# A hybrid mixer layer on one core: the head regrouped into four pairs of channel blocks, with its loads, transposes and low parts reordered

## The reference, cut to what matters

```python
c_act = jax.nn.silu(c)
mod = (c_act @ w_mod + b_mod)[:, None, :]            # 1024 -> 6 x 1024
sh_m, sc_m, gt_m, sh_f, sc_f, gt_f = jnp.split(mod, 6, axis=-1)
h = rms_norm(x, g_pre_mix) * (1.0 + sc_m) + sh_m
y = hybrid_mixer(h, w_in, ...)                       # proj = h @ w_in, 1024 -> 7 x 1024, then conv, LRU, gates, w_o
x = x + gt_m * rms_norm(y, g_post_mix)
# then a squared-ReLU MLP of 4096 channels, treated in the same way
```

## Time and profile before

| what | value |
|---|---|
| runs | 834.62, 836.40, 836.66 us |
| profiled execution | 835.04 us, of which span 833.3 us |
| granted TensorE clock, mean | 0.992 |
| busy: TensorE, weight load, VectorE, ScalarE, GpSimd | 813.3, 701.9, 507.5, 440.0, 28.3 us |
| DMA | 109.52 MB, mean 131 GB/s |

### The profile page before, as it was taken

The page is one execution under the profiler, slowest core; times in us unless marked ns, Lnnn a source line. Parts: engine busy times, 40 slices in busy tenths (PEclk is TensorE's granted clock), DMA queues, the critical chain, the costliest instruction groups (busy, mean ns, idle before and its releaser), DMA issues.

```text
span 833.3 us, 12458 instructions
## 1 busy us (share of the span) xinstructions
PE 813.3 (98%) x4270; PEld 701.9 (84%) x4270; DVE 507.5 (61%) x682; ACT 440.0 (53%) x650; POOL 28.3 (3%) x24
## 2 busy tenths in 40 slices
PE   6799999999999999999999999999999999999997
PEld 6588888888888888888888899999999888888885
DVE  4746677656685565566675579777777533333335
ACT  6356777766674444444334566676767622333332
POOL 1542000000000000000000000000000000000000
PEclk9899999999999999999999999999999999999999
DMA  9942333326077666667337031333333532223302
GB/s 290 348 130 82 107 108 107 107 82 182 26 210 219 181 197 201 189 177 209 129 101 253 1 101 44 109 102 101 101 101 101 177 101 96 85 96 101 101 0 101
DMA packets 134943, 109.52 MB, mean 131 GB/s; under 512 B 4460, under 2 KB 119300, under 8 KB 134916
## 3 DMA queue, kind: packets, MB, share of 16 engines
q1 hardware_dynamic: 134740, 109.10, 43.8%
q10 hardware_dynamic: 144, 0.04, 0.0%
q0 software_dynamic: 32, 0.02, 0.0%
HBM read 107.04 MB, written 2.10 MB: 131 GB/s over the span
## 4 chain that ended last, share of the span: by engine, by line
PE 97%; DVE 1%; ACT 1%; POOL 0%; issue 0%; DMA 0%; DVEq 0%; ACTq 0%
PE ps L416 32%; PE ps L417 31%; PE ps L418 31%; PE ps L1460 1%; PE ps L1471 0%; PE ps L1607 0%; PE ps L1483 0%; POOL ht_lo L600 0%; ACT xnt L657 0%; ACT ht_hi L659 0%; PE ps L1579 0%; PE ps L1580 0%; PE ps L1491 0%; DMA crows<-in_c_dram 0%; DVE sums L1331 0%
## 5 line engine op out<-in xcount | busy, mean ns | idle before, releaser
L416 PE MATMUL ps<-ht_hi,w_hi 128*128 128x512 f32 x448 | 176.9, 395 | 8.0 <-POOL ht_lo L600 5.2
L417 PE MATMUL ps<-ht_lo,w_hi 128*128 128x512 f32 x448 | 175.8, 392 | 0.0
L418 PE MATMUL ps<-ht_hi,w_lo 128*128 128x512 f32 x448 | 175.6, 392 | 0.0
L1020 DVE TENSOR_TENSOR w_lo<-raw,w_hi 128x1024 fp32r<-128x1024 f32 x100 | 122.0, 1224 | 56.7 <-ACT w_hi L630 54.9
L630 ACT ACTIVATE w_hi<-raw 128x1024 fp32r<-128x1024 f32 x96 | 100.4, 1049 | 33.3 <-PE ps L418 28.7
L416 PEld LDWEIGHTS ps<-ht_hi,w_hi 128*128 128x128 f32 x448 | 84.9, 189 | 27.2 <-issue 9.5
L418 PEld LDWEIGHTS ps<-ht_hi,w_lo 128*128 128x128 f32 x448 | 84.9, 190 | 18.0
L417 PEld LDWEIGHTS ps<-ht_lo,w_hi 128*128 128x128 f32 x448 | 85.1, 190 | 17.5
L416 PE MATMUL ps<-w_hi,hd_hi 128*128 128x512 f32 x256 | 99.6, 389 | 0.0
L417 PE MATMUL ps<-w_lo,hd_hi 128*128 128x512 f32 x256 | 99.6, 389 | 0.0
L418 PE MATMUL ps<-w_hi,hd_lo 128*128 128x512 f32 x256 | 99.6, 389 | 0.0
(11 more groups left out here) (227 smaller groups left out, 1492.9 us busy)
## 6 DMA issues: line engine op xcount, KB each, us to landing
raw<-in_w_in_dram SPq DMA_DIRECT2D x48, 512.0 KB, 4.8
modraw<-in_w_mod_dram SPq DMA_DIRECT2D x32, 512.0 KB, 4.0
raw<-in_w_mlp_down_dram SPq DMA_DIRECT2D x32, 512.0 KB, 3.3
up_raw<-in_w_mlp_up_dram SPq DMA_DIRECT2D x56, 256.0 KB, 3.4
mod_raw<-in_w_mod_dram SPq DMA_DIRECT2D x32, 256.0 KB, 7.0
xs<-in_x_dram SPq DMA_DIRECT2D x8, 512.0 KB, 5.3
raw<-in_w_a_out_dram SPq DMA_DIRECT2D x8, 512.0 KB, 5.4
raw<-in_w_b_out_dram SPq DMA_DIRECT2D x8, 512.0 KB, 5.5
```

The source lines that it names most:

```text
L416: nc.tensor.matmul(dst, l_hi, r_hi, start=first, stop=False, skip_group_check=chained)
L417: nc.tensor.matmul(dst, l_hi, r_lo, start=False, stop=False, skip_group_check=chained)
L418: return nc.tensor.matmul(dst, l_lo, r_hi, start=False, stop=last, skip_group_check=chained)
L1020: V.tensor_tensor(w_lo[:, slot, :], raw[:, slot, :], f(w_hi[:, slot, :]), ALU.subtract).then_inc(w_lo_ready, 1)
```

## The change

The groups become four pairs. Every block's unit weights are loaded, rounded and split alone, and lie between the chunks of the modulation. TensorE takes row blocks 0 to 3 of group 0 straight from the chunks, in between the transposes of x, and VectorE 4 to 7. x is first transposed into six banks; blocks 6 and 7 follow in banks 4 and 5 when these have been copied out. Blocks 0 and 1 are modulated straight from PSUM. VectorE makes the low part of the first block of each group. It accumulates a group only when it has finished with the group before. The vectors are all loaded by SP behind x. ScalarE runs a sigmoid and a square root on one column ahead of the data. The unread transposes between tiles go, and 14 come ahead of the first product.

```diff
-    GROUPS = ((0,), (1,), (2, 3), (4, 5), (6, 7))
+    GROUPS = ((0, 1), (2, 3), (4, 5), (6, 7))
+    PE_ROWS = 4
...
+        X_BANKS = 6
+        X_LATE = {6: 4, 7: 5}
...
-                    if g0 == 0 and m0 > 0:
-                        sp_eng.wait_ge(mod0_sum, 1)
+                    if g0 == 0 and m0 < PE_ROWS:
+                        sp_eng.wait_ge(mod0_rows, m0 + num0)
...
             for t in range(TB):
                 sp_eng.dma_start(xs[:, t, :], x_v[:, t, :]).then_inc(xr_in[t], 16)
-                if t == 0:
-                    load_vectors(sp_eng, vectors[1::2], vec_in)
-            load_mod0_group(0)
+            load_vectors(sp_eng, vectors, vec_in)
+            per_group = len(CHUNKS) // len(GROUPS)
+            for c in range(per_group):
+                load_mod0(c)
             load_first_units(0)
-            load_first_units(1)
-            load_mod0_group(1)
-            for g in range(2, len(GROUPS)):
-                load_first_units(g)
-                load_mod0_group(g)
+            for g in range(1, len(GROUPS)):
+                for i in range(per_group):
+                    load_mod0(g * per_group + i)
+                    if i == 1:
+                        load_first_units(GROUPS[g - 1][1])
+                    if i == 2:
+                        load_first_units(GROUPS[g][0])
+            load_first_units(NB - 1)
...
(GpSimd)
             first_units_lo(0)
             pool.wait_ge(h_lo, 1)
+            input_lo(1)
+            first_units_lo(1)
             for g in range(1, len(GROUPS)):
-                first_units_lo(g)
-                for k in GROUPS[g]:
-                    input_lo(k)
+                k0, k1 = GROUPS[g]
+                first_units_lo(k0)
+                pool.wait_ge(h_lo, k0 + 1)
+                input_lo(k1)
+                first_units_lo(k1)
...
(ScalarE)
-            load_vectors(act, vectors[0::2], vec_in)
+            act.wait_ge(const_ready, 4)
+            A(ysum[:, 3 * TB - 1:3 * TB], eps_t[:, 0:1], ACT.Sigmoid)
             act.wait_ge(c_sum, 1)
             A(c_act[:, :], ps[:, B_T0, 0:NB], ACT.Sigmoid).then_inc(sig_c, 1)
-            act.wait_ge(const_ready, 4)
+            A(ysum[:, 3 * TB - 2:3 * TB - 1], eps_t[:, 0:1], ACT.Sqrt)
...
-            act.wait_ge(x_tr, NB)
-            for k in (NB - 1, NB - 2, 0, 1, 2):
-                if k == 1:
-                    first_units_hi(0)
+            act.wait_ge(x_tr, X_BANKS)
+            for k in (4, 5, 2):
                 A(xnt[:, k, :], ps[:, k, :], ACT.Copy).then_inc(xnt_ready, 1)
-            act.wait_ge(xnt_ready, 5)
-            modulate(0, 0)
+            first_units_hi(0)
+            for k in GROUPS[0]:
+                modulate(k, 0)
+            first_units_hi(1)
+            act.wait_ge(xnt_ready, 3)
             act.wait_ge(xnt_ready_dve, 3)
             for g in range(1, len(GROUPS)):
-                first_units_hi(g)
+                first_units_hi(GROUPS[g][0])
                 for k in GROUPS[g]:
                     modulate(k, g)
+                first_units_hi(GROUPS[g][1])
...
(VectorE)
-            accumulate(0, range(NB // 2))
-            dve.wait_ge(x_tr, NB)
-            for k in (3, 4, 5):
-                V.tensor_copy(xnt[:, k, :], ps[:, k, :]).then_inc(xnt_ready_dve, 1)
+            accumulate(0, range(PE_ROWS, NB))
+            dve.wait_ge(x_tr, X_BANKS)
+            V.tensor_copy(xnt[:, 3, :], ps[:, 3, :]).then_inc(xnt_ready_dve, 1)
             dve.wait_ge(cols_ready, 2)
             modulation_columns(0)
-            dve.wait_ge(xnt_ready, 2)
-            accumulate(1, range(0, 2))
-            dve.wait_ge(h_hi, 1)
-            V.tensor_tensor(ht_lo[:, 0, :], xnt[:, 0, :], f(ht_hi[:, 0, :]), ALU.subtract).then_inc(h_lo, 1)
-            accumulate(1, range(2, NB))
+            dve.wait_ge(x_tr, NB - 1)
+            V.tensor_copy(xnt[:, 6, :], ps[:, X_LATE[6], :]).then_inc(xnt_ready_dve, 1)
+            input_lo(0)
+            dve.wait_ge(x_tr, NB)
+            V.tensor_copy(xnt[:, 7, :], ps[:, X_LATE[7], :]).then_inc(xnt_ready_dve, 1)
             for g in range(1, len(GROUPS)):
-                if g + 1 < len(GROUPS):
-                    dve.wait_ge(mod0_acc, acc_count(g, NB - 1))
-                    accumulate(g + 1, range(0, 1))
+                accumulate(g, range(NB))
                 modulation_columns(g)
-                if g + 1 < len(GROUPS):
-                    accumulate(g + 1, range(1, NB))
+                input_lo(GROUPS[g][0])
...
(TensorE)
             for t in range(TB):
                 pe.wait_ge(x_norm, t + 1)
-                for k in range(NB):
+                for k in range(X_BANKS):
...
-                if t < TB - 1:
-                    unread(4)
+                if t == 0:
+                    pe.wait_ge(vec_in, 16 * len(vectors))
+                    nc.tensor.transpose(ps[:, B_T0, P:P + NCOL], vrows[0:NCOL, :], ident[0:NCOL, 0:NCOL]).then_inc(cols_sum, 1)
+                if t == 1:
+                    mod0_direct(range(0, 2))
+            mod0_direct(range(2, PE_ROWS))
+            for k, late in X_LATE.items():
+                pe.wait_ge(xnt_ready, late - 3)
+                for t in range(TB):
+                    last = nc.tensor.transpose(ps[:, late, t * P:(t + 1) * P], xs[:, t, k * P:(k + 1) * P], ident[:, :])
+                last.then_inc(x_tr, 1)
             mod0_columns(0)
-            pe.wait_ge(xnt_ready, 5)
-            pe.wait_ge(xnt_ready_dve, 3)
-            COLUMNS_AT = {(0, 5): 1, (1, 5): 2, (3, 1): 3, (5, 1): 4}
+            pe.wait_ge(xnt_ready, 3)
+            unread(14, ps[:, 2, 0:P])
+            COLUMNS_AT = {(1, 1): 1, (3, 1): 2, (5, 1): 3}
             for k in range(NB):
-                g = next(i for i, ks in enumerate(GROUPS) if k in ks)
-                pe.wait_ge(w0_lo_ready, g + 1)
+                pe.wait_ge(w0_lo_ready, k + 1)
                 pe.wait_ge(h_lo, k + 1)
...
+                    if k == 0 and i == 1:
+                        pe.wait_ge(h_f32, 2)
+                    if k == 0 and i >= 3:
+                        pe.wait_ge(xnt_ready_dve, i - 2)
```

More of the change, by code:

```diff
@@ L220, in hybrid_layer_kernel @@
         raw0_in4 = sem("raw0_in4")
+        raw0_in5 = sem("raw0_in5")
+        raw0_in6 = sem("raw0_in6")
+        raw0_in7 = sem("raw0_in7")
         raw0b_in = sem("raw0b_in")
@@ L250, in hybrid_layer_kernel @@
         xnt_ready_dve = sem("xnt_ready_dve")
+        mod0_rows = sem("mod0_rows")
         mod0_acc = sem("mod0_acc")
@@ L381, in acc_count @@
         def acc_count(g, m):
-            return m + 1 if g == 0 else NB // 2 + NB * (g - 1) + m + 1
+            return NB * g + m + 1 - PE_ROWS
         def col0_count(g):
@@ L1067, in accumulate @@
                         dve.wait_ge(mod0_in[c % M0_BUFS], 32 * (c // M0_BUFS + 1))
-                    if m == 0:
-                        V.tensor_scalar(acc, part, c_act[:, 0:1], None, ALU.mult).then_inc(mod0_acc, 1)
+                    if m == (PE_ROWS if g == 0 else 0):
+                        V.tensor_scalar(acc, part, c_act[:, m:m + 1], None, ALU.mult).then_inc(mod0_acc, 1)
                     else:
@@ L1081, in modulation_columns, with input_lo @@
                                            cols[:, C_GX + k:C_GX + k + 1], ALU.add, ALU.mult).then_inc(col0_ready, 1)
[L1083 to L1086, removed]
-                                   ALU.mult, ALU.min).then_inc(sp_step, 1)
-            V.tensor_scalar(cols[:, C_BC:C_BC + NB], cols[:, C_BC:C_BC + NB], 1.0, None, ALU.add).then_inc(cols_ready, 1)
+            def input_lo(k):
+                dve.wait_ge(h_hi, k + 1)
+                V.tensor_tensor(ht_lo[:, k, :], xnt[:, k, :], f(ht_hi[:, k, :]), ALU.subtract).then_inc(h_lo, 1)
             for t in range(TB):
@@ L1456, in _, with unread, mod0_columns @@
             nc.tensor.transpose(ps[:, B_T0, 0:NB], crows[:, :], ident[0:NB, 0:NB]).then_inc(c_sum, 1)
-            def unread(count):
+            def unread(count, dst):
                 for _ in range(count):
-                    nc.tensor.transpose(ps[:, NB // 2, (TB - 1) * P:], ident[:, :], ident[:, :])
-            unread(24)
-            pe.wait_ge(vec_in, 16 * len(vectors))
-            nc.tensor.transpose(ps[:, B_T1, 0:NCOL], vrows[0:NCOL, :], ident[0:NCOL, 0:NCOL]).then_inc(cols_sum, 1)
+                    nc.tensor.transpose(dst, ident[:, :], ident[:, :])
+            def mod0_direct(blocks):
+                for m in blocks:
+                    c = CHUNK_OF[0, m]
+                    if m == CHUNKS[c][1]:
+                        pe.wait_ge(mod0_in[c], 32)
+                    for a in range(2):
+                        for k in GROUPS[0]:
[3 more added lines that the diff above has]
+                    last.then_inc(mod0_rows, 1)
+            def mod0_columns(g):
+                pe.wait_ge(mod0_acc, acc_count(g, NB - 1))
+                for k in GROUPS[g]:
+                    for a in range(2):
```

(43 more changed lines are left out.)

50 lines of the change are left out of this document (23 added, 27 removed).

## The result

The changed kernel takes 842.0 us (median of 4, 841.14 to 844.49) against 835.53 beside it: ratio 1.008, 95% interval 1.0056 to 1.0103. It is slower by 6.5 us by the medians; forecast were 829.5 and a gain of 6.1. The profiled execution took 841.14 us, span 839.3, against 835.04 and 833.3, so there are 6.0 us of span to find.

The account below looks back on a forecast made before the run. TensorE, busy 98%, bounds the kernel, so only its head counts: ending at 60.3 instead of 66.43 us, it gains 6.1. 835.0 - 6.1 = 828.9, or 830.3 off the median; predicted 829.5 us, range 826.5 to 834.0.

Parts of the forecast that it names:

- I cost all of that at nothing ... the cover is the loads.: Ahead of the first product: early sigmoid and root and ScalarE's fewer DMA issues cost nothing, hidden behind the loads.
- x's chain, 10.4 + 1.9 + 1.4 + 1.9 + 0.9 = 16.5: TensorE's front: first chunk, direct products, two tiles, direct products, late transposes, done at 16.5 us.
- The clock rival: In the head's products: half clock through block 0 and again at groups 2 and 3, gain 3.3, 832.3 us; 12%.
- the slack of block 1: TensorE waits 2.3 us for group 1 after block 1's unit 0; half clock at block 0 falls into it.
- less work for TensorE: In x's front: six transposes for eight and no unread ones between tiles mean less TensorE work.
- The sum of group 0's columns: Start of the head: VectorE ends accumulating row blocks 6 and 7 at 16.5 us and the sum follows.
- the loads, held to be the limit: Ahead of the first product: 4.3 MB for group 0's last chunk, landing at 14.9 us, 14.3 to 15.5.
- The loop: From accumulated group through sum, columns, modulate, round and low part: 3.7 us; first product 20.2 to 20.3, head's end 60.3.
- The turn of 10.2 us: In the head, VectorE sets the pace: accumulation 6.5 plus 3.7 gives 10.2 us a group, against TensorE's 9.0.
- The cover behind the head: At the gates: VectorE's chain moves 5.7 us earlier, TensorE 6.1; 0.5 us is left, without it a few tenths lost.
- The slower rival: In the new loop: GpSimd's work holds VectorE up, up to 4.8 us a turn, 8.3 slower, 843.3 us; 5%.

Follow-up runs that it names:

- experiment 4: The kernel before with all eleven vectors loaded by SP behind x, nothing else of the change: 843.9 us, ratio 1.0075.
- experiment 1: vec_split: the changed kernel with the small vectors loaded as before, half by SP behind x's first tile, half by ScalarE: 839.06 us, ratio 1.0022.
- experiment 6: The changed kernel with 16 more unread transposes at the start and four put back between x's tiles: 839.44 us, ratio 1.0032.
- experiment 9: The version that beats both: changed kernel, vectors loaded as before, GpSimd's memset late, 28 more unread transposes, GpSimd making first blocks' low parts (groups 1 to 3): 829.72 us.
- experiment 3: The changed kernel with the vectors loaded as before and GpSimd's memset held back until VectorE's softplus steps are over: 833.1 us, ratio 0.9965.
- experiments 8: On the kernel of experiment 3, GpSimd again makes the low part of the first block of groups 1 to 3: 835.07 us, ratio 0.9966.
- experiment 2: The changed kernel with GpSimd's 3.5 us memset held back until VectorE's softplus steps are over, nothing else: 837.35 us, ratio 1.0001.
- experiment 10: On the kernel of experiment 9, VectorE instead of GpSimd makes the low part of block 7's weights: 830.12 us, ratio 0.9917.
- warm_front: On the kernel of experiment 3, 16 more unread transposes at the start and four put back between x's tiles: 832.68 us, ratio 0.9948.

## Why the prediction was wrong

By its own steps:

- **"I cost all of that at nothing ... the cover is the loads."** This is the first step that failed. It read the vectors' move only as SP's issue order and ScalarE's relief. SP's queue got eleven issues (2.61 to 6.8 us) between x and the modulation, the last vector landed 4.8 us after its issue, and TensorE and VectorE wait for it in order, in front of the second and third tiles of x. The text asked what stood behind the first narrow matmuls, not what stood behind `vec_in`. The edit alone costs 6.3 us in the kernel before (experiment 4); in the changed kernel taking it back gains 4.8 us by the ratios (experiment 1), most of it, as it seems at equal clock, because the clock is then low less often.
- **x's chain, 10.4 + 1.9 + 1.4 + 1.9 + 0.9 = 16.5.** The chain measured is 12.2 + 2.7 + 2.7 + 3.2 + 1.8 = 22.7. 1.8 is the later begin; 4.3 is half clock, which lengthened every term. The clock rival was put at the products, where the slack of block 1 would have hidden it. It struck ahead of them, where nothing hides it. The text priced the unread transposes that the change removes as "less work for TensorE"; 28 put back, 12 of them between the tiles, gain 4.0 us on the changed kernel (experiment 6). What the 12 do alone no run shows. And the chain was short even so: in the version of experiment 9, with the vectors early and the clock at 1.00, TensorE reaches the sum at 18.29, 1.8 us after the forecast 16.5, because its first narrow matmuls begin at 11.75 instead of 10.4 and the unread transposes are in the queue.
- **The sum of group 0's columns** was put at the end of the accumulation (16.5). VectorE ended it at 18.51. With the vectors moved back it ended at 17.07 (experiment 3), so 1.4 of the 2.0 us are the vectors' too: SP asks for the first chunk at 6.82 us with them in front, and at 4.30 without. The remaining 0.6 stay open. But TensorE's queue reached the sum at 22.66 only, so the loads, held to be the limit, had 4 us of slack. In vec_split and its kin the start is TensorE's queue too; only with VectorE's accumulation does it change sides.
- **The loop was right.** From the first product to the first whole unit 40.0 us were forecast and 66.94 - 27.02 = 39.9 measured. The turn of 10.2 us is there, in VectorE's timeline of the changed kernel, from group 1's columns to group 3's:

```profile
35.01 0.16 DVE L1090 TENSOR_TENSOR mcol<-ps,cols 128x2 f32<-128x2 f32 x1 [1.15 <-PE ps L1492]
...
55.41 0.16 DVE L1090 TENSOR_TENSOR mcol<-ps,cols 128x2 f32<-128x2 f32 x1 [1.15 <-PE ps L1492]
```

(55.41 - 35.01) / 2 = 10.2. That half clock at block 0 would fall into the wait for group 1 was right too: that wait was 0.53 us, with 2.3 forecast at full clock. That VectorE sets the turn, and that its own low part is what makes it so, was shown by experiments 8 and 9: given back to GpSimd, the turn is 9.3 us and the kernel some 2.5 us faster. So VectorE's low part of each group's first block, a part of the change, costs time in this loop.
- **The cover behind the head, "0.5 us is left ... a few tenths would be lost".** It was 1.1 us short even with the memset held back. This is the second step that failed. It moved the two subtractions earlier at their old 2.62 us; beside GpSimd's extra instruction for block 7 they take 3.75. And the step didn't ask what GpSimd does there: the memset is released by TensorE's sixth unit, the softplus steps by VectorE's own queue, and in the change the second came later than the first. That is 2.7 us and the half clock behind it (1.6).
- **The slower rival** had the right pair of engines and the wrong place. Beside GpSimd the accumulation steps in the loop stay at 0.75 us, as the earlier trace rows said, and VectorE's low part in the loop (0.69) has no GpSimd work beside it. Two other VectorE instructions, behind the loop, were held up: the first subtraction of raw0b and the softplus step.

What stays open: why the clock falls in one execution of a kernel and not in the next. The comparisons at equal clock rest on a few runs each, and the profiled executions don't sit at the medians.

## What to carry to other kernels

A wait is priced by everything that is queued behind it on its engine, so every DMA that moves in a queue has to be followed to the instruction that waits for it, however small the data. Work that nobody reads can be what keeps TensorE's clock up (4.0 us here): where a change removes some, price the queue behind it at half clock too, and look for low clock ahead of the bulk of the products, not only in it. Where runs scatter, compare them at equal granted clock before giving a gain to an edit. When one engine's work moves by some microseconds against another's, list the instructions of both that may now overlap, the memsets too.

## What the runs showed of the hardware

- **A GpSimd memset stops some VectorE instructions and not others.** Within the 3.52 us memset, a SCALAR_TENSOR_TENSOR of 128x8 at 67.67 took 0.17 us, and the TENSOR_SCALAR of 128x8 behind it 2.84, to the memset's end. Held back behind the softplus steps (experiment 2), the memset leaves that TENSOR_SCALAR at 0.17. In the kernel before, three SCALAR_TENSOR_TENSORs of 128x512 beside its memset took 2.32 us and a subtraction of 128x1024 1.22, as without one. The Trainium skill (GPSIMD Engine Reference, "Key points") says that VectorE's two-port modes contend with GpSimd. The 2.84 us against 0.17 fit that; that the TENSOR_SCALAR ran in such a mode no trace shows.
- **VectorE's subtraction with two inputs in SBUF waits for GpSimd's, and GpSimd's isn't slowed.** On VectorE 2.61 us for the one that begins during GpSimd's and 1.21 for the next (experiment 10), 1.40 lost in 1.53 beside it; in the kernel of experiment 9 2.54 and 1.21. GpSimd's takes 1.84 us beside VectorE's and 1.81 with VectorE idle (at 20.07). Beside a memset VectorE's isn't held up, as the 1.22 above shows.
- **Half clock held through 14 us of unbroken work.** From 13 to 27 us TensorE was busy for 14.00 of 14.00 us, with matmuls of one output column and with 128x128 transposes, and the granted clock stayed at 0.50, the 1.2 GHz level. 16 narrow matmul instructions took 3.4 us there and 1.84 at full clock. In the version that beats both, with 28 more unread transposes among the same work and the vectors early, the profiled execution stayed at 1.00 from some 8 to 40 us. That isn't sure to happen: in warm_front, with the same transposes, no wait of TensorE from 9.1 to 13.3 us was over 0.20 us, and the clock was 0.50 from 13.7 to 16.3 all the same.
- **The granted clock at the very start isn't what the windows print.** They give 1.00 from 0 us, but the unread transposes at the start come every 0.21 us at first and every 0.11 later, as the timeline of the version that beats both shows (windows 6:7 and 8.2:9.2):

```profile
5.61 1.70 PE L1475 MATMUL ps<-ident 128*128 128x128 f32 x7
...
7.96 1.45 PE L1475 MATMUL ps<-ident 128*128 128x128 f32 x11
```

The first is the pace of the lower level, and it lasts to about 8 us.
